# A ring of seven weight units with the rests written over them, decays broadcast by DMA, and chains of small steps spaced wider

## What is computed

```python
def reference(...):
    x = first_block(x, ...)      # layer 0: LRU + mLSTM; layer 1: SSD; RMS norm at the end
    return second_block(x, ...)  # S5 + gated linear attention + differential attention,
                                 # a gated sum, w_out, a conv-gated MLP, RMS norm
```

## Time and profile before

| | |
|---|---|
| Three runs | 3530.93 us median, 3530.44 to 3531.49 |
| The profiled execution's own time | 3531.95 us |
| Its span, first to last instruction | 3530.1 us |
| Mean granted TensorE clock | 0.968 of full |
| TensorE busy | 3290.6 us (93%) |
| VectorE / ScalarE / GpSimd busy | 2315.8 / 1798.8 / 672.7 us |
| HBM traffic | 552 MB, mean 156 GB/s |
| First loads, in order | vec 543.5 KB, x 512 KB, shp 516 KB, w_if 576 KB, unit 0 512 KB, x 512 KB twice, unit 1, x, units 2, 3 |

### The profile page before, as it was taken

How to read it: one execution, slowest core, us unless ns; L and a number is a source line. 1 busy time by engine, 2 the same in 40 slices (tenths; PEclk the granted TensorE clock), 3 DMA queues, 4 the chain that set the end, 5 groups by cost and what they waited for, 6 DMA issues and landing times.

```text
span 3530.1 us, 54486 instructions
## 1 busy us (share of the span) xinstructions
PE 3290.6 (93%) x21902; PEld 2961.2 (84%) x21902; DVE 2315.8 (66%) x3229; ACT 1798.8 (51%) x2313; POOL 672.7 (19%) x1118
## 2 busy tenths in 40 slices
PE   6999878999999999999889888989999999999998
PEld 5889777889888888888878777878999888888887
DVE  6655766656666666576666666666556788888544
ACT  4444666544555555544455444333444566666443
POOL 1000000010000000011567765885000100000000
PEclk9999988999999999999999998999999999999999
DMA  4445333655434344455433333344655655555554
GB/s 169 155 136 169 112 114 122 204 190 187 136 131 131 132 132 137 164 182 196 163 109 114 114 114 107 127 132 147 206 185 173 197 191 190 190 189 190 186 191 142
DMA packets 148749, 552.08 MB, mean 156 GB/s; under 512 B 16512, under 2 KB 16512, under 8 KB 147856
## 3 DMA queue, kind: packets, MB, share of 16 engines
q1 hardware_dynamic: 148496, 548.61, 46.9%
HBM read 542.25 MB, written 6.29 MB: 155 GB/s over the span
## 4 chain that ended last, share of the span: by engine, by line
PE 72%; DVE 10%; POOL 8%; ACT 6%; issue 2%; DMA 1%; SPq 0%; DVEq 0%; ACTq 0%; POOLq 0%
PE ps L543 72%; POOL TB L1909 4%; DVE WL L1313 2%; POOL PT L1909 2%; ACT L880 2%; ACT WH L890 1%; POOL BX L1909 1%; POOL SQ L1909 1%; POOL BS L1909 1%; ACT SQ L880 1%; DMA RAW<-in_w 0%; DVE XC L1287 0%; DVE X L1287 0%; DVE BS L1303 0%; DMA scratch<-X 0%
## 5 line engine op out<-in xcount | busy, mean ns | idle before, releaser
L543 PE MATMUL ps<-XN,WH 128*128 128x256 f32 (+1 forms) x8864 | 1900.7, 308 | 78.3 <-DVE WL L1313 31.1
L890 ACT ACTIVATE WH<-RAW 128x1024 fp32r<-128x1024 f32 x1010 | 1064.3, 1057 | 1391.5 <-PE ps L543 1349.8
L1313 DVE TENSOR_TENSOR WL<-RAW,WH 128x1024 fp32r<-128x1024 f32 x1010 | 1253.1, 1244 | 566.6 <-ACT WH L890 559.9
L543 PEld LDWEIGHTS ps<-XN,WH 128*128 128x128 f32 x8864 | 1463.6, 196 | 184.0 <-issue 47.9
L543 PE MATMUL ps<-XN,WL 128*128 128x256 f32 x5120 | 1459.7, 285 | 0.0
L543 PEld LDWEIGHTS ps<-XN,WL 128*128 128x128 f32 x5120 | 997.5, 195 | 0.0
L543 PE MATMUL ps<-YS,WH 128*128 128x512 f32 (+1 forms) x1088 | 374.9, 390 | 10.3 <-DVE ZB L1276 6.0
L1909 POOL TENSOR_TENSOR RSB<-RSB,SQ 128x256 f32<-128x256 f32 x75 | 86.6, 1154 | 1341.8 <-ACT SQ L880 1340.8
L543 PE MATMUL ps<-YS,WL 128*128 128x256 f32 x1056 | 295.6, 280 | 0.0
L543 PEld LDWEIGHTS ps<-YS,WH 128*128 128x128 f32 x1088 | 202.8, 189 | 58.9 <-DVE ZB L1276 7.1
L1909 POOL TENSOR_TENSOR SQ<-SQ 128x256 f32<-128x256 f32 (+1 forms) x32 | 33.6, 1051 | 1144.8 <-ACT SQ L880 1143.3
(11 more groups left out here) (332 smaller groups left out, 3482.9 us busy)
## 6 DMA issues: line engine op xcount, KB each, us to landing
RAW<-in_w SPq DMA_DIRECT2D x1010, 512.0 KB, 3.4
scratch<-X SPq DMA_DIRECT2D x2, 2048.0 KB, 7.4
X<-scratch SPq DMA_DIRECT2D x2, 2048.0 KB, 8.6
X<-in_x SPq DMA_DIRECT2D x4, 512.0 KB, 9.0
X<-in_x SPq DMA_DIRECT2D x1, 2048.0 KB, 10.4
out<-X SPq DMA_DIRECT2D x4, 512.0 KB, 2.6
WIF<-in_w_if SPq DMA_DIRECT2D x1, 576.0 KB, 7.0
CV<-in_vec SPq DMA_DIRECT2D x1, 543.5 KB, 3.9
```

The costliest lines, as they stand in the source:

```text
L543: return pe.e.matmul(dst, l, r, start=start, stop=stop, skip_group_check=True)
L890: act.e.activation(WH[:, w % NW, :], RAW[:, w % NRAW, :], ACT.Copy).then_inc(*act.one(("wh", w)))
L1313: dve.e.tensor_tensor(WL[:, w % NW, :], RAW[:, w % NRAW, :], WH[:, w % NW, :].bitcast(F32), SUB).then_inc(*dve.one(("wl", w)))
```

## The change

- `RAW` becomes a ring of 7 (`NB`), and `WL` lies at the same addresses: VectorE writes the rest of a unit over its raw weights. `WH` is a ring of 5 (`NH`). Twelve unit buffers in all, as before.
- At `unit(u)` ScalarE splits unit u + 4 and VectorE writes the rest of u + 3, both one further ahead. At u = 0 ScalarE splits only units 0 and 1, VectorE rests only unit 0, and both catch up by two units at a time (`ahead`).
- SyncE loads unit u + 6 at `unit(u)` as before, but waits for TensorE to be through with unit u - 1, where it waited for the rest of unit u + 2.
- First loads: vec, x, unit 0, x, unit 1, shp, x, unit 2, x, units 3 to 6, w_if. The waits for shp move behind the first tiles.
- SSD: no broadcast matmuls. The running sums (64 rows of 256) are stored to DRAM, and per head one DMA on SyncE's queue broadcasts a row to 128 partitions (`csb`, a ring of 5). ScalarE writes two Relu with a bias and one Exp over 384 columns for the two Exp. The mask goes into CBm: VectorE multiplies the scores by a triangle of ones, where ScalarE copied them. All steps behind come one step earlier, 16 in all.
- Spacing: heads 12 to 16 steps a head, gla 14 to 18, diff 10 to 15, S5 pairs 10 to 11 apart (181 to 197 steps). End diff(h - 2) takes the place of End diff(h - 1), with End diff(2) behind the last Go. The g12, gb and db tiles come in pairs of n, and End diff(3) stands behind four g12 and two gb.

```diff
-NRAW = 4
-NW = 4
+NB = 7
+NH = 5
+AHEAD = 4
+NCSB = 5
...
+def ahead(u, n):
+    done = min(2 * u + n - AHEAD, u + n) if u else 0
+    return range(done, min(2 * u + 2 + n - AHEAD, u + n + 1, NUNITS))
...
-        RAW = v3(fx("RAW", NRAW * UB * 128), NRAW)
-        WH = v3(fx("WH", NW * UB * 128, F32R), NW)
-        WL = v3(fx("WL", NW * UB * 128, F32R), NW)
+        RAW = v3(fx("RAW", NB * UB * 128), NB)
+        WL = v3(Map(nc, base, end)("WL", NB * UB * 128, F32R), NB)
+        WH = v3(fx("WH", NH * UB * 128, F32R), NH)
...
             def unit(u):
-                for w in range(u + NW - 1 if u else 0, min(u + NW, NUNITS)):
-                    act.wait_ge(raw_in[w % NRAW], 16 * (w // NRAW + 1))
-                    if w >= NW:
-                        act.wait_ge(*at("used", w - NW))
+                for w in ahead(u, AHEAD):
+                    act.wait_ge(raw_in[w % NB], 16 * (w // NB + 1))
+                    if w >= NH:
+                        act.wait_ge(*at("used", w - NH))
...
             def unit(u):
-                for w in range(u + NW - 2 if u else 0, min(u + NW - 1, NUNITS)):
-                    sp.wait_ge(*at("wl", w))
-                    raw(w + NRAW)
+                if u:
+                    sp.wait_ge(*at("used", u - 1))
+                    raw(u - 1 + NB)
...
-                    mm(b[:, 0:384], identr, maskr, True, False)
-                    mm(b[:, 0:384], ident[0:64, h:h + 1].to_broadcast([64, 128]), CSX, False, True).then_inc(
-                        *pe.one(("bc", g, e_)))
...
-                    fn(d[:, 0:256], b[:, 0:256], ACT.Exp, bias=NCST[:, h:h + 1])
-                    fn(d[:, 256:384], b[:, 256:384], ACT.Exp, ("dec_", g, e_), ("free", "bc", g, e_),
-                       bias=NCST[:, 64 + h:65 + h])
+                    fn(d[:, 0:256], b, ACT.Relu, bias=CST[:, h:h + 1], scale=-1.0)
+                    fn(d[:, 256:384], b[:, 128:256], ACT.Relu, ("csr", g, e_), bias=CST[:, 64 + h:65 + h], scale=-1.0)
+                    fn(d, d, ACT.Exp, ("dec_", g, e_), scale=-1.0)
...
+            def csb(h):
+                if h < 64:
+                    sp.e.dma_start(CSB[h % NCSB], sums[h:h + 1, :].to_broadcast([128, 256])).then_inc(csb_in[h % NCSB], 16)
+            def dts(s):
+                if s == 4:
+                    sp.wait_ge(*at("csx"))
+                    load(sums, CSX, "cst")
+                if s == 5:
+                    sp.wait_ge(*at("cst"))
+                    sp.wait_ge(*at("st1"))
+                    for h in range(NCSB):
+                        csb(h)
+            def ssd(g, s):
+                if 1 <= s <= 8:
+                    e_ = s - 1
+                    sp.wait_ge(*at("csr", g, e_))
+                    csb(8 * g + e_ + NCSB)
...
     for n in range(32):
-        r = s - (10 + 10 * (n // 2) + 5 * (n % 2))
+        r = s - (11 + 11 * (n // 2) + 5 * (n % 2))
```

More of the change, by code:

```diff
@@ L172, in plan @@
             p += [End("gla", (2,)), End("gla", (3,)), End("lam", ()), Now("dbl", ())]
-        else:
-            p.append(End("diff", (h - 1,)))
+        elif h > 1:
+            p.append(End("diff", (h - 2,)))
         p.append(Go("diff", (h,)))
[L176 to L179, removed]
+    p.append(End("diff", (2,)))
+    for m in range(0, 16, 2):
+        for n in (m, m + 1):
+            for c in range(2):
+                p.append(whole(tile("g12", (n, c), "w_in_2", 7184 + 2048 * (c + 1) + 128 * n), 16))
+        for n in (m, m + 1):
+            p.append(whole(tile("gb", (n,), "gla_w_br_2", 128 * n, "gos"), 8))
+        if m == 0:
             p.append(End("diff", (3,)))
-        p.append(whole(tile("gb", (n,), "gla_w_br_2", 128 * n, "gos"), 8))
-        p.append(whole(tile("db", (n,), "diff_w_br_2", 128 * n, "dos"), 8))
+        for n in (m, m + 1):
+            p.append(whole(tile("db", (n,), "diff_w_br_2", 128 * n, "dos"), 8))
     for n in range(16):
@@ L330, in flat, with build @@
     return ap.rearrange("p a b -> p (a b)")
-def build(nc, args, out, scratch):
+def build(nc, args, out, scratch, sums):
     ctx = ExitStack()
@@ L415, in build @@
         XV1 = v3(m("XV1", 6 * 256), 6)
+        CSB = [m(f"CSB{i}", 256) for i in range(NCSB)]
         assert m.at <= XT + 2048
@@ L492, in build @@
         sp_none = sem("sp_none")
-        raw_in = [sem(f"raw_in{i}") for i in range(NRAW)]
-        loads = ["cv", "cs", "wif", "x1", "st1", "x2", "st2", "b1", "b2", "c1", "c2", "wg", "db", "x3"]
+        raw_in = [sem(f"raw_in{i}") for i in range(NB)]
+        csb_in = [sem(f"csb_in{i}") for i in range(NCSB)]
+        loads = ["cst", "cv", "cs", "wif", "x1", "st1", "x2", "st2", "b1", "b2", "c1", "c2", "wg", "db", "x3"]
         loads += [f"x0{q}" for q in range(4)]
@@ L1559, in zs @@
             def zs(g, j, s):
+                if g == 0 and j == 0:
+                    dve.wait_ge(*at("cst"))
                 evac(ZB[:, j, :], 1, "zs", g, j, more=[("zsr", g)])
@@ L1572, in ssd @@
                            bank("xt", g, t).rearrange("p (h d) -> p h d", h=8), d, MUL, ("free", "xt", g, t))
-                if 3 <= s <= 10:
-                    e_ = s - 3
+                    dve.wait_ge(*at("cb", g))
+                    tt(CBm, bank("cb", g)[:, 0:384], TRI, MUL, ("free", "cb", g))
+                if 2 <= s <= 9:
+                    e_ = s - 2
                     dve.wait_ge(*at("dec_", g, e_))
-                    dve.wait_ge(*at("cbm", g))
                     tt(DB[e_ % 3], DB[e_ % 3], CBm, MUL, ("msk", g, e_))
-                if s == 12:
+                if s == 11:
                     if g:
@@ L2063, in sync @@
             x0(0)
-            load(CS, args["shp"], "cs")
-            load(WIF, args["w_if"], "wif")
             raw(0)
             x0(1)
+            raw(1)
+            load(CS, args["shp"], "cs")
             x0(2)
-            raw(1)
+            raw(2)
             x0(3)
-            raw(2)
             raw(3)
+            raw(4)
+            raw(5)
+            raw(6)
+            load(WIF, args["w_if"], "wif")
             walk(lambda t, k, a, b: None, unit, {
-                "x1": x1, "st1": st1, "x2": x2, "s5l": s5l, "st2": st2, "wg": wg, "dbl": dbl, "x3": x3, "last": last})
+                "x1": x1, "st1": st1, "dts": dts, "ssd": ssd, "x2": x2, "s5l": s5l, "st2": st2, "wg": wg, "dbl": dbl, "x3": x3, "last": last})
         for engine in (tensor, scalar, vector, gpsimd, sync):
@@ L2195, in program @@
     scratch = nc.dram_tensor("scratch_0", (128, 16, 256), F32).ap()
-    build(nc, args, out, scratch)
+    sums = nc.dram_tensor("sums_0", (64, 256), F32).ap()
+    build(nc, args, out, scratch, sums)
 def kernel(**inputs):
```

170 lines of the change are left out of this document (77 added, 93 removed), and 6 rows, old and new, of the table STEPS.

## The result

| | before | after |
|---|---|---|
| Median of the runs | 3530.73 us (4 runs) | 3475.43 us (4 runs, 3474.76 to 3475.68) |
| Span of the profiled execution | 3530.1 us | 3472.6 us |
| Mean granted clock | 0.968 | 0.959 |
| TensorE busy | 3290.6 us | 3231.7 us |

The ratio is 0.9843 (0.9826 to 0.986): faster, as forecast, by 55 us where I had 159. 3475 lies outside the range of 3312 to 3440. No rival gave this number: what I expected to win in SSD was there and about half of it was given back, and part of the spacing cost time.

The account below looks back on a forecast made before the run. Mostly matmuls bound it, the rest being matmuls that wait on latency in chains, with GpSimd bounding late S5. Terms summed to -159 us, from 3531.95 less 1 to 3372 us; 8 in 10 range 3312 to 3440.

Parts of the forecast that it names:

- The SSD term: SSD groups: broadcast matmuls leave TensorE, 8.4 us a group over 8 groups; -67 us (-58 to -70).
- The end of S5: Last S5 stretch: pairs 11 apart put 11 units into GpSimd's 40.8 us period; -4 us (-20 to +12).
- My forced ends: Within the S5 term: ending diff(2) with seven steps left and diff(3) with five costs 15 us.
- Heads: LRU stretch with mLSTM heads: 16 steps win a third of 84 us of idle and low clock; -28 (-10 to -45).
- rival (a): LRU, GLA, diff and S5: spacing only moves the waits, these stretches keep their times; 3448 us, chance 0.2.
- GLA: GLA stretch: wider spacing wins two thirds of 18 us of idle and low clock; -12 us (0 to -16).
- Diff: Diff stretch: spacing removes scores' waits and most squares' waits, 60% of 55 us; -33 us (-12 to -48).
- Cover: Waits for rests outside the LRU stretch: one unit more bridges 2.88 us per burst; -11 us (-3 to -18).
- Start: Kernel start: earlier unit loads and fewer splits put the first matmul near 12.5 us; -8 us (-4 to -9).
- Gates: First gate tile: S5's last steps end right at it, so gg waits; +4 us (0 to +8).
- (c): SSD heads: Relu needs another table than Exp, two table loads per head; +75 us, 3447 us, chance 0.03.
- (d): SyncE's queue in SSD: broadcasts delay weight loads, making the kernel slower; 3560 us at y = 3, chance 0.03.

Follow-up runs that it names:

- The last kernel: Changed kernel with SSD's tail later, S5 pairs 10 apart, no End diff(2), diff's sum of squares on VectorE, SSD's sum matmul later still: 3391.43 us, ratio 0.9606.

## Why the prediction was wrong, and where it was right

The sum had 159 us and 55 came. By the rows SSD with oo is 30 us short, the heads 19, S5 19, GLA 12, cover 9, diff 8 and the start 4.

**The SSD term, -67: the price was right and a sentence behind it was wrong.** Where a broadcast stood beside the head's own matmuls, units went from 4.87 to 3.85 us, and where it stood alone from 4.07 to 2.88. The Exp of 384 columns took 0.52 us, for 0.5 assumed. The step that failed is "The waits for GpSimd's squares in each group keep their distance in steps, and stay." The distance among the chain's own steps stayed. The distance to the tile evacuations, which have a period of two units, did not, and the waits went from 2.2 to 4.3 us with low clock behind them, 35 us in seven groups. With the tail moved back by a step the SSD and oo rows together took 764 us, 60 less than before; with the sum's matmul later still, 741, 84 less, which is more than the term, as the squares' waits that it left in place went too.

**The end of S5, -4 where it was +15.** I wrote "With 11 units it needs 36.3 us, and GpSimd remains the bound", with 40.8 us a pair, and got 43 to 45. The size of GpSimd's work was about right: with pairs 10 apart, where it has hardly a pause, late tables come 39.9 to 41.2 us apart. Whether the eleventh rest adds the 0.9 us that I took is open: without the pauses a period is 38.7 to 39.9 us in the changed kernel, and 39.8 to 41.8 with the input matmuls ahead. What failed is that it would have no pauses: TensorE's order in a step, HH's wait ahead of the next input, took overlap away. With the order set right the row took 372 us: of the 19 us by which it missed its forecast, 12 came of the order. The periods were still 41.4 to 42.3 us; what makes them longer than 40.8 is not shown. I counted steps between a writer and its reader, and not which waits share a step. So a unit cost 4.0 us as before the change, not 3.7, and 16 more of them lie under S5: the 99 units took 396 us, where the sum had 374. My forced ends were 15 us for both; they cost 11.4 (in the diff row) and 14.9, so 26: diff's squares stood in GpSimd's queue behind S5's tables.

**Heads, -28, got -9** (-11 in the heads' stretch, +2 in eo). "I take a third of the 84 us" was the step that failed: no row gave that share. The waits for the heads' squares (9.8 us in this stretch) and most of those for EB (8.4 to 2.1) went, as forecast. VectorE's evacuation of the z tiles took their place (6.0 to 29.4 us). That is rival (a) for this stretch alone. Less work on VectorE gave 9 us, so its queue is part of the cause; why it is so late was not tried.

**GLA, -12, got 0.** Its own spacing is worth 6 us; S5's 11 steps cost 8 there. **Diff, -33, got -25**: the scores' waits went, one forced end came (11.4 us).

**Cover, -11, got about -2.** 14.7 us of waits for rests went, but 8.0 of them in the LRU stretch, which had its own term. At S5's constants (u) 2.9 us went, a unit's time as forecast, and the row has it. In the first convolutions 1.5 us went, but the waits for Q grew from 6.1 to 7.8 us and the one for XMP from 1.4 to 2.8, and the rows of xm to z kept their 278 us. A unit more of cover for one wait was not time where another wait of the same stretch grew by as much.

**Start, -8, got -4.** TensorE begins at 13.00 us, for 12.5 forecast and 20.75 before. (Unit 0 was there at 7.8 us; the proportion of which I wrote gives 6.2, not 7.) But the eight units behind it took 40 us, not 36. "The matmuls then wait no longer than they waited before" was wrong: TensorE, early, waits for the norms that wait for x and units 2 and 3.

**Gates, +4, got +3**, the wait for ZS 3.0 us.

**The rivals.** (c) is out: 153 table loads, 152 before; by the Trainium skill, ScalarE: Activation LUTs, section Table sets, relu is in every set, and the trace agrees. (d) is out: a broadcast lands 3.7 us after its issue, a weight load still after 3.3 us. (a), at 3448 the nearest, has the waits moved but not worse; what happened in S5 is worse. The last kernel, at 3391.43, is 140 us under the one before, but it took five more edits, and 17 of these us (84 less 67) are more than the sum had in SSD. So most of the time was there to win, but not by this change.

## What to carry to other kernels

When a step moves by one unit, write down beside it everything else on its engine with a period of its own (tile ends, other chains), and look at which of these it now meets; the distance to its own chain's neighbours is half of the question. When a spacing changes, look for two operations that come to share a step, and put the one that starts the next round ahead of the one that waits. And a chain that is ended by force waits for the longest queue that it passes through: an add of 0.7 us behind another chain's table cost TensorE 14 us.

## What the runs showed of the hardware

What a wait for the squares did to the granted clock of the unit behind it, in the SSD stage (0.5 is the 1.2 GHz level, values between are a mix of both levels):

| Wait | Kernel | Clock in the unit behind |
|---|---|---|
| 2.2 to 2.3 us | before | 1.00 in seven groups |
| 2.0 us | before, last group | 0.68 |
| 1.9 to 2.1 us | changed, tail one step later | 1.00 in two groups, 0.62 to 0.68 in six |
| 4.3 us | changed | 0.62 in one group, 0.50 to 0.54 in six |
| 1.9 us | changed, last group | 1.00 |
| 4.4 us | before, tail one step later | 0.63 to 0.72 in seven groups |

So the length of the wait alone does not tell the clock behind it; what else decides was not tried. In the changed kernel 2.1 us more of wait came with some 2.5 us more behind it.

VectorE and GpSimd slow each other, which my sum had for BX alone. Two rests beside GpSimd's adds of the heads' squares took 3.43 us, and 2.35 without them in the kernel before (VectorE then GpSimd, in the changed kernel):

```profile
435.20 3.43 DVE L1309 TENSOR_TENSOR WL<-RAW,WH 128x1024 fp32r<-128x1024 f32 x2
...
435.89 3.31 POOL L1906 TENSOR_TENSOR SQ<-SQ 128x512 f32<-128x512 f32 x2 [67.01 <-ACT SQ L880]
```

Three instructions of a convolution took 2.91 us beside such adds in the kernel before, 1.53 alone; and GpSimd's adds took 2.79 us where they began beside a rest, 2.07 to 2.26 where they began beside an evacuation or a convolution, and 2.06 with VectorE idle. The Trainium skill, in SBUF - State Buffer, section Who interferes with whom, has a VectorE instruction with two inputs in SBUF contend with GpSimd; the rows agree. Adding to VectorE's queue to spare GpSimd still lost, since the queue weighed more than the speed.
